# A decoder step on one core: how the feed-forward input products divide 520 columns between two matmuls

## What is computed

```
D_MODEL = 1024
D_FF = -(-8 * D_MODEL // (3 * 256)) * 256      # 2816
...
    def ffn(u, li):
        gate, up = jnp.split(u @ w_ffn_in[li], 2, axis=-1)
        return (jax.nn.silu(gate) * up) @ w_ffn_out[li]
...
        up = xp * (1.0 + mod_p[4]) + mod_p[3]
        us = xs * (1.0 + mod_s[4]) + mod_s[3]
        xp = post_norm(xp, ffn(up, li), mod_p[5], li, 1)
        xs = post_norm(xs, ffn(us, li), mod_s[5], li, 1)
```

## Time and profile before

| | |
|---|---|
| median of three runs | 1642.11 us |
| the profiled execution | 1640.14 us |
| its span, first to last instruction | 1638.3 us |
| mean granted TensorE clock | 0.921 of full |
| HBM read, written | 168.01 MB, 5.63 MB |

### The profile page before, as it was taken

One profiled execution on the slowest core, in us unless ns is written; L12 is line 12 of the kernel. 1 busy time (PEld: TensorE's weight loads), 2 busy tenths in 40 slices (PEclk: granted clock), 3 DMA queues, 4 the chain that ended last, 5 costly groups with the idle time before them and its releaser, 6 DMA issues.

```text
span 1638.3 us, 28976 instructions
## 1 busy us (share of the span) xinstructions
PE 1437.3 (88%) x12160; PEld 1374.8 (84%) x12160; DVE 786.0 (48%) x1148; ACT 501.7 (31%) x623; POOL 260.0 (16%) x202
## 2 busy tenths in 40 slices
PE   5799988976778699999999779797959999999994
PEld 4799966663778699999999769797949999999993
DVE  2623247775464733333333577479573323333345
ACT  0311243233022522212222254683243322222222
POOL 2000020002035100000002422813530000000043
PEclk8899988985569899999999989899989999999996
DMA  9431397766412132243313301311422223432201
GB/s 327 153 103 53 98 351 256 249 206 171 116 27 78 52 92 65 72 121 104 95 57 94 116 14 40 129 49 49 114 76 78 73 68 105 124 83 79 71 19 53
DMA packets 215613, 175.18 MB, mean 107 GB/s; under 512 B 8903, under 2 KB 184764, under 8 KB 215364
## 3 DMA queue, kind: packets, MB, share of 16 engines
q1 hardware_dynamic: 213520, 169.72, 33.6%
q0 software_dynamic: 1840, 3.79, 0.8%
q10 hardware_dynamic: 140, 0.09, 0.0%
HBM read 168.01 MB, written 5.63 MB: 106 GB/s over the span
## 4 chain that ended last, share of the span: by engine, by line
PE 71%; DVE 16%; issue 4%; ACT 3%; DMA 3%; POOL 2%; SPq 1%; DVEq 0%; ACTq 0%; POOLq 0%
PE ps L2049 56%; PE ps L2068 5%; DVE wlo L1474 2%; PE ps L1994 2%; PE ps L2125 2%; DVE nb L1588 1%; DVE xc L1726 1%; DVE UL L1581 1%; DMA raw<-in_w_ada 1%; DVE ub L1603 1%; DVE rstd L1648 1%; DVE cmB L1251 1%; ACT whi L934 1%; DMA xtok<-in_x_prompt 1%; DMA raw<-in_w_in_even 1%
## 5 line engine op out<-in xcount | busy, mean ns | idle before, releaser
L2049 PE MATMUL ps<-UH,whi 128*128 128x260 f32 x1936 | 392.6, 284 | 13.7 <-DVE wlo L1474 13.7
L2049 PE MATMUL ps<-UH,wlo 128*128 128x260 f32 x1936 | 392.7, 285 | 0.0
L2049 PE MATMUL ps<-UL,whi 128*128 128x260 f32 x1936 | 391.8, 284 | 0.0
L934 ACT ACTIVATE whi<-raw 128x2048 fp32r<-128x2048 f32 (+3 forms) x115 | 193.8, 1686 | 555.0 <-PE ps L2049 515.3
L2049 PEld LDWEIGHTS ps<-UH,whi 128*128 128x128 f32 x1936 | 300.8, 190 | 15.0 <-DVE wlo L1474 15.0
L1474 DVE TENSOR_TENSOR wlo<-raw,whi 128x2048 fp32r<-128x2048 f32 (+3 forms) x115 | 252.9, 2200 | 102.6 <-ACT whi L934 102.1
L2049 PEld LDWEIGHTS ps<-UH,wlo 128*128 128x128 f32 x1936 | 300.8, 190 | 0.0
L2049 PEld LDWEIGHTS ps<-UL,whi 128*128 128x128 f32 x1936 | 299.8, 190 | 0.0
L1659 DVE TENSOR_TENSOR hb<-ps,silb 128x520 f32<-128x520 f32 x44 | 30.8, 700 | 281.0 <-PE ps L2049 260.1
L2049 PE MATMUL ps<-HH,wlo 128*128 128x260 f32 x616 | 124.3, 283 | 0.0
L2049 PE MATMUL ps<-HL,whi 128*128 128x260 f32 x616 | 124.2, 283 | 0.0
(11 more groups left out here) (423 smaller groups left out, 2060.5 us busy)
## 6 DMA issues: line engine op xcount, KB each, us to landing
raw<-in_w_ada SPq DMA_DIRECT2D x96, 512.0 KB, 6.8
raw<-in_w_ffn_in SPq DMA_DIRECT2D x88, 512.0 KB, 4.8
raw<-in_w_in_even SPq DMA_DIRECT2D x24, 512.0 KB, 4.6
raw<-in_w_ffn_out SPq DMA_DIRECT2D x32, 384.0 KB, 3.9
raw<-in_w_ffn_out SPq DMA_DIRECT2D x32, 320.0 KB, 3.3
raw<-in_w_in_odd SPq DMA_DIRECT2D x20, 512.0 KB, 4.4
raw<-in_w_out_odd SPq DMA_DIRECT2D x16, 320.0 KB, 3.5
raw<-in_w_out_even SPq DMA_DIRECT2D x8, 512.0 KB, 7.9
```

What stands on the lines that cost most here:

```text
L934: ins = nc.scalar.activation(whi[w % 2][:, 0:f], raw[c % NRAW][:, 0:f], ACT.Identity)
L2049: ins = T.matmul(ps(g)[:, hf, 0:HT], wt[:, k, wc], x[:, k, hf], start=(k == 0 and wt is wh and x is xh), stop=(k == s.k - 1 and wt is wl_))
```

## The change

In the ten chunks of each input stage that go through `products`, the two matmuls of a term no longer take 260 and 260 columns. One takes the 512 prompt columns into the first bank of the group, the other the 8 sample columns into the second. It applies to stages whose name begins with `fi`; the first chunk, through `gemm`, keeps its layout. ScalarE and VectorE read these groups with one instruction for the samples and one for the prompt, and write `silb` and `hb` in the layout as before.

```
--- before.py
+++ after.py
@@ -998,7 +998,11 @@
                         wait_filled(act, g)
                         if k >= 2:
                             act.wait_ge(h_ready, k - 1)
-                        ins = nc.scalar.activation(silb[c % 2][:], pT(g), ACT.Silu)
+                        if c == 0:
+                            ins = nc.scalar.activation(silb[0][:], pT(g), ACT.Silu)
+                        else:
+                            nc.scalar.activation(smpl(silb[c % 2]), ps(g)[:, 1, 0:NS].rearrange("p (a b) -> p a b", a=2), ACT.Silu)
+                            ins = nc.scalar.activation(tok(silb[c % 2]), ps(g)[:, 0].rearrange("p (a b) -> p a b", a=2), ACT.Silu)
                         free(ins, g)
                         act.wait_ge(freed[g % NGRP], g // NGRP + 1)
                         if c < s.n - 1:
@@ -1656,7 +1660,13 @@
                         wait_filled(dve, g)
 
                         dve.wait_ge(freed[(g - 1) % NGRP], (g - 1) // NGRP + 1)
-                        v.tensor_tensor(hb[c % 2][:], pT(g), silb[c % 2][:], ALU.mult).then_inc(h_ready, 1)
+                        if c == 0:
+                            v.tensor_tensor(hb[0][:], pT(g), silb[0][:], ALU.mult).then_inc(h_ready, 1)
+                        else:
+                            v.tensor_tensor(smpl(hb[c % 2]), ps(g)[:, 1, 0:NS].rearrange("p (a b) -> p a b", a=2),
+                                            smpl(silb[c % 2]), ALU.mult)
+                            v.tensor_tensor(tok(hb[c % 2]), ps(g)[:, 0].rearrange("p (a b) -> p a b", a=2), tok(silb[c % 2]),
+                                            ALU.mult).then_inc(h_ready, 1)
                         settled(dve, h_ready)
                         dve.wait_ge(h_ready, k + 1)
                         free(v.tensor_copy(sml[0:1, 4:5], ps(g)[0:1, 0, 0:1]), g)
@@ -2045,9 +2055,15 @@
                     for k in range(s.k):
                         wc = slice(m * P, (m + 1) * P)
                         for wt, x in ((wh, xh), (wh, xl), (wl_, xh)):
-                            for hf in range(2):
-                                ins = T.matmul(ps(g)[:, hf, 0:HT], wt[:, k, wc], x[:, k, hf], start=(k == 0 and wt is wh and x is xh),
-                                               stop=(k == s.k - 1 and wt is wl_))
+                            first, last = k == 0 and wt is wh and x is xh, k == s.k - 1 and wt is wl_
+                            if s.name[:2] == "fi":
+                                T.matmul(ps(g)[:, 0].rearrange("p (a b) -> p a b", a=2), wt[:, k, wc], tok(x[:, k]),
+                                         start=first, stop=last)
+                                ins = T.matmul(ps(g)[:, 1, 0:NS].rearrange("p (a b) -> p a b", a=2), wt[:, k, wc], smpl(x[:, k]),
+                                               start=first, stop=last)
+                            else:
+                                for hf in range(2):
+                                    ins = T.matmul(ps(g)[:, hf, 0:HT], wt[:, k, wc], x[:, k, hf], start=first, stop=last)
                     done(ins)
 
             def gemm(name, xh, xl, ready, n_ready):
```

## The result

The changed kernel takes 1840.3 us in the median of four runs, against 1641.9 us of the kernel before on the same chip: a ratio of 1.1207, 95% interval 1.1184 to 1.1231. It is slower by 198 us; the forecast was 1810 us with a range of 1785 to 1862.

The account below looks back on a forecast made before the run. TensorE's products in the four input stages were taken to bound the kernel. Pairs go from 240.3 to 216 + 111 = 327.5 ns, +87 ns x 1920 = +167 us, giving 1810 us, range 1785 to 1862.

Parts of the forecast that it names:

- The mechanism: Input-stage pairs: the next 512-column product's load begins only with the 8-column product and lies bare; +87 ns per pair, 84%.
- The load's term: Bare weight load of the 512-column product, once per pair: 111 ns, between 100 and 120.
- The stream's term: Streaming 512 split-type columns in each input-stage pair: 216 ns, scaled from 110 ns for 260; between 213 and 237.
- The upper bound in the forecast: Highest price for streaming 512 columns in a pair: the present pace scaled, 512/260 x 120.1 = 237 ns.
- the signs that the forecast named: Input stages: pieces of 157 us, groups filled in 7.9 us, starts alternating 216 and 111 ns, granted clock 1.00.
- the tests of the whole argument: Wrong if loads start twice within a 512-column stream, the clock there shows half, or over 12160 products are counted.
- The 8x512 rows: Split-type 512-column products in the earlier trace, at half clock: at most 0.47 us each, 0.237 at full clock; cited as support.
- What was costed at nothing: One more ScalarE and VectorE instruction in each of 40 chunks, covered by waiting for TensorE; 15 us if uncovered.
- Both loads under the long stream: Rival for the input-stage pairs: both loads fetched under the 512 columns, 222 ns per pair, -35 us, 1607 us; 7%.
- The short product for an issue slot: Rival: the 8-column product costs only an issue slot, its load vanishes; pair 236 to 240 ns, 1642 us; 4%.
- The clock: Rival: TensorE's clock falls to half in the input stages, a pair takes some 650 ns, +790 us; 3%.
- The 8-column product as a plain one: Rival: it is lowered to two instructions with a load each, +111 ns more per pair, 2020 us; 2%.

## Why the prediction was right, and what was off

**The mechanism held.** The forecast was that the next long load can begin only with the short product and lies bare. The timelines show it so, doubling the short product adds one more such load, and shortening the short product's own load brings nothing. That the load of the long product is the one paid rests on the timelines and on the products with loads of 8 columns; no run shortened that load.

**The load's term:** 111 ns taken, 112 measured (two short products against one), between its bounds of 100 and 120. The 1 ns is worth 2 us.

**The stream's term was mis-sized.** I took 216 ns for 512 columns by scaling plain products of 260 columns, 110 ns being half of the 220 that one of them takes. The pair's 343.2 ns less 112 leaves 231 ns. The missing 15 ns x 1920 = 29 us are nearly the whole difference between the forecast of 1810 and 1840 us. The step that was off is "In plain products nothing but the stream shows, so I take 110 ns for 260 columns of the split kind": the split kind has a pace of its own at full clock, about 0.45 to 0.46 ns per column at every width tried, against 0.42 for one column per clock. The upper bound in the forecast, the present pace scaled, gave 237 ns and was the nearer. I had read the 10 ns over the stream in today's 120.1 as a hand-over between products and let it vanish in a long one; 512 columns with the load hidden, 232.5 ns, show that it grows with the columns. The measured time still fell inside the range because that upper bound was taken into it. Two of the signs that the forecast named did not come as written: the pieces are 164.7 us and not 157, and the starts do not alternate 216 and 111 ns but, by the records, 316 and 27, since a long product's record starts well before its stream. By its own test (wrong if the long products come near 237 ns) the step on the stream is nearer to wrong than to right, with 231; the tests of the whole argument (two loads under one stream, half clock, more than 12160 products) all came out for it.

**The 8x512 rows did not decide it**, since they stood at half clock. At half clock the split products show no excess. The timeline of before, products of 260 columns at a granted clock of 0.50:

```profile
1118.33 0.64 PE L2049 MATMUL ps<-UL,whi 128*128 128x260 f32 x2
1118.76 0.64 PE L2049 MATMUL ps<-UH,wlo 128*128 128x260 f32 x2
1119.19 0.64 PE L2049 MATMUL ps<-UH,whi 128*128 128x260 f32 x2
```

Starts of neighbouring pairs are 0.43 to 0.44 us apart, 216 ns each, which is 260 columns at 1.2 GHz. A stream measured at half clock must not simply be halved.

**What was costed at nothing cost nothing.** The readers: ratio 1.0001 with the added instructions on 260 columns each. The stage's end, by the timeline of VectorE for the last chunk:

```profile
729.72 0.17 DVE L1666 TENSOR_TENSOR hb<-ps,silb 128x8 f32<-128x8 f32 x1 [12.61 <-PE ps L2062]
...
731.32 0.70 DVE L1677 TENSOR_TENSOR HL<-hb,HH 128x520 fp32r<-128x520 f32 x1 [0.58 <-ACT HH L1013]
732.74 1.63 DVE L1478 TENSOR_TENSOR wlo<-raw,whi 128x1408 fp32r<-128x1408 f32 x1 [0.72 <-ACT whi L934]
```

The low part of `hb` is done at 732.0, 2.5 us after the last group, and the low weights at 734.4, against a piece of 8 us that begins at 729.5; the same slack as in the earlier trace rows.

**The rivals.** Both loads under the long stream: no, in every timeline shown here one load is taken ahead. The short product for an issue slot: the trace of after does show the record of a long product starting 0.03 us after the short one's, and a reader who trusted that start would take the short product for cheap. The pair's 343 ns and the next load's start show that the record begins before the stream does. The Trainium skill's floor of about 25 ns for 1 to 64 columns (TensorE: Matmul & The Clock Gate, "Back-to-back issue gap"), which that section gives for products without a budget for their loads, holds in the changed kernel for the start of the record alone. For the pair, 343 ns against the estimate of 241, it is out by 100 ns. The clock: it stayed at 1.00 in the changed kernel, but the grouped form, with the same products in another order, shows that this rival was a real one. The 8-column product as a plain one: the count stayed at 12160.

## What to carry to other kernels

Where every matmul brings its own weight load of 128 columns, divide a row of columns so that no product is shorter than a load. Here a load is about 112 ns, by an estimate from 0.46 ns per column the time of some 240 columns; 260 and 260 was the fastest division of the 520 columns that was tried. Eight columns cost as much here as some 240 would, so spread a small remainder evenly over the products rather than giving it one of its own. And price a stream from rows of the same operand type at the same clock: here the type was worth 7% of the stream, 29 us of 198.

## What was not expected of the hardware

At full clock, products of the split (fp32r) type took 0.45 to 0.46 ns per column (231 ns for 512, 180 for 390, 138 for 300, 120 for 260), where plain ones took 220 ns for 260; at a granted clock of 0.50 the split type took 216 ns for 260, one column per clock of 1.2 GHz. The excess over one column per clock did not change with a shorter load under the stream, with other weights, or without the gap in the columns. What sets it is open.

Twenty-four products of 8 columns on end, 2.6 us in which TensorE is busy by its records, were followed by stretches at the lower clock level, which made the four stages 89 us longer; twelve on end were not.
